# A hybrid decoder step on one core: input loads, chunk order, gelus and state decay put in other places

## The chip, the cores and the metric

The kernel runs on one core of a Trainium2 chip. The metric is the device time of one execution in microseconds; the kernel before took 1114.2 us, the median of three runs (1113.9 to 1114.36). The engines named here are TensorE (PE, matmuls), VectorE (DVE), ScalarE (ACT), GpSimd (POOL) and SyncE (SP, which issues most transfers). They run side by side, each in its own order of instructions, and wait for each other by semaphores.

## The reference

One decoder layer over 536 tokens: 16 meta tokens and 512 prompt tokens of one sequence, and one new token for each of 8 running samples. All of it is float32.

```python
xn = rmsnorm(x);  proj = xn @ w_in                  # columns z (1024), xbc (1536), dt (16), u (1024)
xbc = silu(causal_conv(xbc));  dt = softplus(dt + dt_bias)
# SSD group: 16 heads of 64, state 128, chunks of 128 tokens
for chunk c:
    y_diag = ((C B^T) * exp(segment sums) * dt) @ x  # inside the chunk
    y_off  = (C @ H) * exp(cumulated decay)          # from the state H before the chunk
    H      = decay_of_chunk * H + B^T @ (decayed x)
y_ssd = rmsnorm((y_diag + y_off + D x) * silu(z))
# S5 group: 64 groups of 16 channels, complex diagonal state of 64
y = gelu(Re(C h) + D u);  y = y * sigmoid(y @ w_glu + b_glu);  y_s5 = rmsnorm(y)
x = x + concat(y_ssd, y_s5) @ w_out
x = x + experts(rmsnorm(x))                          # 32 SwiGLU experts, two per token in one of 4 groups
y = rmsnorm(x)                                       # and the new states
```

The states of the eight samples are updated too: each is multiplied by its decay, gets an outer product added, and is read out against C.

## The kernel before, in words

**Wide blocks.** The input projection and the first S5 gate (GLU) are 36 blocks of 128 output features over all 536 tokens, `wide(0)` to `wide(35)`: 0 to 7 make u, 8 to 19 make xbc, 20 to 27 make z, and 28 to 35 multiply the gelu output `yg` by `w_glu`. A block is 64 float32 matmuls (recorded as x32), takes its weights (512 KB) from one of three ring buffers, which `ring_load(w)` on SP fills once block w-3 is done, and writes two PSUM banks, which ScalarE then empties (`wide_free`). Blocks 20 to 27 all use banks 0 and 1; from block 28 on even ones use 0 and 1, odd ones 2 and 3.

**S5.** Eight tokens are done at a time through a Toeplitz matrix `Tm` of 64 groups. It is assembled by 32 small SP transfers, `toeplitz(r)` for r = 0 to 3 with eight pieces each (L406). GpSimd runs the recurrence over 66 steps meanwhile (L553 to L564, end marked by `h_done`). `state_outputs(first, n)` on TensorE (L768) then makes n rounds of four groups in PSUM banks 2 and 3, and VectorE adds each to the rest of y (L1651, `y5_ev`); round r waits for the addition of round r-2. Because y has another layout than the gate needs, SP stores it to `y_scr` in HBM, in two halves of nine transfers (`y_store`, L432), and loads it back (`y_load`, L436). Then ScalarE takes the gelus (L1209) and TensorE may begin block 28, tile by tile.

**SSD.** Each of five chunks (the last has 16 tokens) has four parts on TensorE: `ssd_a` (transposes L779, L781 and C B^T, L783), `ssd_b` (segment sums, L794, in banks 2 and 3), `ssd_y_off` (C @ H, L802) and `ssd_c` (y and the new state, L815 to L824). ScalarE takes `b_tokens`, then the exponentials `segment_exp` (L1176). VectorE scales the off-diagonal part (L1624, `yo_ev`), multiplies the masks (L1629), adds y (L1636, `y_ev`) and then decays the state `Hs` and adds to it (L1646, `st_ev`).

**Samples.** When the last state output is done, GpSimd loads 2 MB of rows of B and C and eight states of 512 KB (L576, L578). For each sample VectorE makes the product with C and its sum (`sample_c`, L1608); only then may GpSimd overwrite the state (L586, L587) and store it (L591).

**Out-projection and experts.** y is split into a high and a low float32r part (L1690); `project_block` (L911) starts when the gate blocks are out of PSUM and the low part of `y_ssd` is made. SP issues the first experts' weights on counts of the out-projection. Routing follows, then 32 experts whose 6 MB each stream through three buffers.

All orders are written out by hand, as the order of calls on each engine. Those around the change are the SP list (L409 to L448), the TensorE list from `ssd_b(0)` to `wide(35)` (L829 to L866), the ScalarE loop over chunks with the gelus behind it (L1197 to L1214) and the VectorE loop over chunks (L1611 to L1657).

Of the kernel before, what the change touches and what calls it, by code (L numbers as in the profile page):

```python
# [38 lines left out]
NP_ = META + SEQ  # L39
# [41 lines left out]
def build(nc, a):  # L81
    ctx = ExitStack()
    with ctx:
# [268 lines left out]
        def _(sp):  # L352
# [58 lines left out]
            toeplitz(0)  # L411
            toeplitz(1)
            ring_load(14)
            toeplitz(2)
            toeplitz(3)
            for w in range(15, 22):
                ring_load(w)
# [22 lines left out]
            for w in range(26, 29):  # L440
                ring_load(w)
# [5 lines left out]
            for w in range(29, 31):  # L447
                ring_load(w)  # L448
# [180 lines left out]
        def _(pe):  # L629
# [214 lines left out]
            wide(24)  # L844
            state_outputs(0, 8)
            ssd_a(2)
# [10 lines left out]
            wide(26)  # L857
            ssd_c(3)
            wide(27)
# [3 lines left out]
            wide(28)  # L863
            ssd_c(4)
            for w in range(29, 36):
                wide(w)  # L866
# [170 lines left out]
        def _(ac):  # L1037
# [159 lines left out]
            for c in range(5):  # L1197
                b_tokens(c)
                if c:
                    segment_exp(c)  # L1200
                if c < 4:
                    decays(c + 1)
                for w in ((21, 22), (23, 24), (25,), (26, 27), ())[c]:
                    z_evac(w)

            for i in range(8):
                if i % 4 == 0:
                    ac.wait_ge(yraw_ld[i // 4], 16)
                act_(yg[:, i, 0:NP_].rearrange("p (m j) -> p m j", j=J),  # L1209
                     yraw[:, i, 0:NP_].rearrange("p (j m) -> p m j", j=J), ACT.Gelu_apprx_tanh)  # L1210
                act_(yg[:, i, NP_:N], yraw[:, i, NP_:N], ACT.Gelu_apprx_tanh).then_inc(gelu_done, 1)
            for i in range(2):
                ac.wait_ge(wide_free[i], 14)
# [149 lines left out]
        def _(dv):  # L1363
# [9 lines left out]
            def tt(o, x, y, op):  # L1373
                link(V.tensor_tensor(o, x, y, op))  # L1374
# [237 lines left out]
            for c in range(5):  # L1612
# [9 lines left out]
                for g in range(2) if c else ():  # L1622
# [3 lines left out]
                                    bc(dE[0:n, c, 0, 8 * g:8 * g + 8], 2, HD), ALU.mult).then_inc(yo_ev, 1)  # L1626
                for g in range(2):
# [3 lines left out]
                if c == 4:  # L1631
                    sample_c(2)
                    sample_c(3)
# [6 lines left out]
                for g in range(2):  # L1640
# [3 lines left out]
                    else:  # L1644
                        tt(hs, hs, bc(dE[:, c, 1, 8 * g:8 * g + 8], 2, HD), ALU.mult)
# [7 lines left out]
                if c == 3:  # L1653
                    sample_c(0)
                    sample_c(1)
            for b in range(4, NS):
                sample_c(b)  # L1657
# [322 lines left out]
```

## Time and profile before

| what | us |
|---|---|
| median of three runs | 1114.2 |
| profiled execution | 1111.12 |
| its span | 1109.3 |
| TensorE busy in it | 995.4 (90%) |
| VectorE busy | 440.9 (40%) |
| ScalarE busy | 310.7 (28%) |
| GpSimd busy | 329.9 (30%) |
| mean granted TensorE clock | 0.961 of full speed |

The profile is of one execution. Its times are counted from the start of the span. Busy shares are means over the whole span, in which the stages differ: the last half (from 588 us on) is the experts, the first half the layer's two head groups and the out-projection. Register, branch and semaphore instructions are not counted as busy, and a few matmul records may be missing.

### The profile page before, as it was taken

To read this page: it belongs to the slowest core of one execution; us is meant where nothing else is said; L and a number is where in the kernel's file an instruction comes from. 1 tells how busy PE (TensorE), PEld (TensorE's weight loads), DVE (VectorE), ACT (ScalarE), POOL (GpSimd) and SP (SyncE) were. 2 spreads that over 40 slices of the span, in tenths; PEclk is the share of its full clock that TensorE was granted. 3 is DMA by queue.
4 is the path that set the end of the run, shared out by engine and by line. 5 is a ranking of instruction groups with operands and counts; after the bars stand their busy time and mean duration, and the time that the engine had idled before them with its cause. 6 is when DMAs were issued, how large, how long until landed. Compare 5 with 4: busy or idle time off the path is not lost.

```text
span 1109.3 us, 17059 instructions
## 1 busy us (share of the span) xinstructions
PE 995.4 (90%) x6472; PEld 708.7 (64%) x6473; DVE 440.9 (40%) x673; ACT 310.7 (28%) x595; POOL 329.9 (30%) x534
## 2 busy tenths in 40 slices
PE   6999989999999999999889999999987687998881
PEld 5889769786776788898676555555544344554440
DVE  6999874534345699952331111111111011111103
ACT  3025223543312535411312222222211211221223
POOL 1000888888023992000002222222222121221210
PEclk9999999999979899999959999999999999999996
DMA  7683261110629734346369999999999999999964
GB/s 266 121 144 67 49 133 39 39 60 22 104 84 267 237 123 151 106 191 264 141 246 324 396 400 367 351 390 398 397 395 409 388 419 412 411 418 415 423 278 161
DMA packets 73564, 277.54 MB, mean 250 GB/s; under 512 B 36952, under 2 KB 38872, under 8 KB 56496
## 3 DMA queue, kind: packets, MB, share of 16 engines
q1 hardware_dynamic: 63020, 252.67, 62.4%
q0 software_dynamic: 8720, 19.86, 6.5%
q10 hardware_dynamic: 1780, 4.41, 1.1%
q8 instruction: 29, 0.48, 0.2%
q14 instruction: 15, 0.12, 0.0%
HBM read 260.17 MB, written 25.61 MB: 258 GB/s over the span
## 4 chain that ended last, share of the span: by engine, by line
PE 51%; DMA 22%; DVE 18%; SPq 5%; issue 2%; ACT 1%; POOLq 0%; ACTq 0%; POOL 0%; DVEq 0%
DMA sb_arena<-w_up 19%; PE ps L649 9%; PE ps L1005 9%; PE ps L1019 7%; DVE sb_arena L1374 7%; PE ps L998 7%; PE ps L911 6%; SPq L406 2%; SPq L432 2%; PE ps L963 2%; PE ps L979 2%; PE ps L768 2%; PE ps L737 1%; PE ps L819 1%; DVE sb_arena L1506 1%
## 5 line engine op out<-in xcount | busy, mean ns | idle before, releaser
L649 PE MATMUL ps<-sb_arena 128*128 128x264 f32 (+1 forms) x1152 | 271.7, 396 | 15.7 <-DVE sb_arena L1417 8.9
L649 PEld LDWEIGHTS ps<-sb_arena 128*128 128x128 f32 x1152 | 221.1, 193 | 66.6 <-DMA sb_arena<-wi 13.8
L1875 DVE TENSOR_TENSOR sb_s5b<-sb_s5b,ps 128x256 f32<-128x256 f32 x36 | 22.4, 622 | 411.2 <-PE ps L1005 411.2
L1005 PE MATMUL ps<-sb_arena 128*64 128x256 f32 x1152 | 136.2, 391 | 21.2 <-DMA sb_arena<-w_up 21.2
L1019 PE MATMUL ps<-sb_arena 128*64 128x512 f32 x576 | 131.5, 598 | 20.5 <-DVE sb_arena L1879 20.5
L998 PE MATMUL ps<-sb_arena 128*64 128x256 f32 x1152 | 131.0, 380 | 15.8 <-DMA sb_arena<-w_gate 12.3
L998 PEld LDWEIGHTS ps<-sb_arena 128*64 128x64 f32 x1152 | 82.9, 137 | 74.4 <-DMA sb_arena<-w_gate 20.9
L1005 PEld LDWEIGHTS ps<-sb_arena 128*64 128x64 f32 x1152 | 84.3, 141 | 69.3 <-DMA sb_arena<-w_up 27.5
L1347 ACT ACTIVATE sb_kxf<-ps,sb_gate_of 64x512 f32<-64x512 f32 x36 | 24.6, 682 | 306.6 <-PE ps L1019 306.6
L1019 PEld LDWEIGHTS ps<-sb_arena 128*64 128x64 f32 x576 | 39.0, 136 | 89.9 <-issue 61.0
L605 POOL COPY sb_idc<-sb_tok_of 64x1 int32 x36 | 6.4, 177 | 281.0 <-DMA sum_scr<-sb_kxf,sb_rwc 249.6
L1374 DVE TENSOR_TENSOR sb_arena<-sb_arena 128x64 f32<-128x64 f32 (+12 forms) x86 | 83.2, 968 | 5.5 <-ACT sb_arena L1048 1.9
L616 POOL DMA_INDIRECT sum_scr<-sb_kxf,sb_rwc x36 | 52.6, 1460 | 30.4 <-POOL sb_rwc L613 30.4
L911 PE MATMUL ps<-sb_y_hi,sb_wo_hi 128*128 128x268 f32 x256 | 53.9, 292 | 4.8 <-DVE sb_arena L1743 2.6
L911 PE MATMUL ps<-sb_y_lo,sb_wo_hi 128*128 128x268 f32 x256 | 52.4, 286 | 0.0
L911 PE MATMUL ps<-sb_y_hi,sb_wo_lo 128*128 128x268 f32 x256 | 52.3, 286 | 0.0
L596 POOL DMA_INDIRECT sb_arena<-x_scr,sb_tok_of x4 | 3.8, 960 | 161.9 <-DVE sb_tok_of L1865 161.0
L911 PEld LDWEIGHTS ps<-sb_y_hi,sb_wo_hi 128*128 128x128 f32 x256 | 39.9, 188 | 8.8 <-issue 5.5
L608 POOL DMA_INDIRECT sb_arena<-x_scr,sb_idc x36 | 34.8, 968 | 30.2 <-POOL sb_idc L605 28.6
L979 PEld LDWEIGHTS ps<-sb_cst,sb_arena 64*128 64x128 f32 x288 | 34.5, 200 | 13.8 <-issue 13.8
L911 PEld LDWEIGHTS ps<-sb_y_lo,sb_wo_hi 128*128 128x128 f32 x256 | 39.9, 188 | 0.0
L911 PEld LDWEIGHTS ps<-sb_y_hi,sb_wo_lo 128*128 128x128 f32 x256 | 39.8, 188 | 0.0
(301 smaller groups left out, 1292.2 us busy)
## 6 DMA issues: line engine op xcount, KB each, us to landing
sb_arena<-w_gate SPq DMA_DIRECT2D x32, 2048.0 KB, 30.2
sb_arena<-w_up SPq DMA_DIRECT2D x32, 2048.0 KB, 32.8
sb_arena<-w_down SPq DMA_DIRECT2D x32, 2048.0 KB, 32.6
sb_arena<-wi SPq DMA_DIRECT2D x28, 512.0 KB, 4.0
sb_arena<-w_out SPq DMA_DIRECT2D x4, 2048.0 KB, 8.3
sb_arena<-wglu SPq DMA_DIRECT2D x8, 512.0 KB, 4.3
sb_arena<-ssm_in POOLq DMA_DIRECT2D x8, 512.0 KB, 15.4
o_ssm_s<-sb_arena POOLq DMA_DIRECT2D x8, 512.0 KB, 5.1
```

The lines of the kernel that those rows point to most:

```text
L406: sp.dma_start(Tm[16 * j:16 * j + 16, r::4, j:J, :], Kx[32 * r:32 * r + 16, :, 0:J - j, :]).then_inc(t_ld, 16)
L608: nc.gpsimd.indirect_dma_start(xg[u], None, x_scr, bass.IndirectOffsetOnAxis(ap=idc[u], axis=0), bounds_check=N - 1, oob_is_err=False).the ...
L616: nc.gpsimd.indirect_dma_start(sum_scr, bass.IndirectOffsetOnAxis(ap=rwc[u % 2], axis=0), yo[u % 2], None, bounds_check=N - 1, oob_is_err= ...
L649: last = mm(ps[:, b0 + h, 0:t1 - t0], ring[w % 3][:, k, :], src[:, k, t0:t1], start=k == 0, stop=k == KD - 1)
L911: last = mm(ps[:, 2 * (o % 2) + h, 0:HALF], w_[:, k, c:c + P], y_[:, k, HALF * h:HALF * h + HALF], start=k == 0 and j == 0, stop=k == KD - ...
L979: last = nc.tensor.transpose(ps[:, 2, k * T:(k + 1) * T], rows_[:, k::KD], cst[0:T, C_ID:C_ID + T])
L998: last = mm(ps[64 * r:64 * r + 64, 0, 0:256], xt[:, k, :], Wg[s][:, k, 256 * r:256 * r + 256], start=k == 0, stop=k == KD - 1)
L1005: last = mm(ps[64 * r:64 * r + 64, 1, 0:256], xt[:, k, :], Wu[s][:, k, 256 * r:256 * r + 256], start=k == 0, stop=k == KD - 1)
L1019: last = mm(ps[64 * r:64 * r + 64, 4, :], ht[:, k % 2, 64 * (k // 2):64 * (k // 2) + 64], Wd[s][:, k, 512 * r:512 * r + 512], start=k == 0 ...
L1347: act_(yo[u % 2][:, 0:512], ps[0:64, 4, :], ACT.Copy, scale=gate_of[0:64, bass.ds(q, 1)])
L1374: link(V.tensor_tensor(o, x, y, op))
L1875: V.tensor_tensor(hh.rearrange("p (j c) -> p c j", j=2), sg.rearrange("p (c j) -> p c j", j=2), ps[:, 1, 0:256].rearrange("p (c j) -> p c ...
```

## The change

SP issues the loads of blocks 14 and 15 between Toeplitz rounds, and that of block 28 behind the second y store and both y loads. TensorE does chunk 2's `ssd_a` ahead of the first state outputs, block 27 ahead of chunk 3's `ssd_c`, block 28 ahead of all of chunk 4, and block 29 ahead of chunk 4's `ssd_c`, with a wait for both scaled off-diagonal parts since block 29 writes their banks. ScalarE does chunk 4's `b_tokens` and exponentials behind the gelus, and the gelus read contiguously and write with stride, where they read with stride and wrote contiguously. VectorE decays each half of the state as soon as its off-diagonal part is scaled, and does the samples' products in other places: 0 to 2 in chunk 3 ahead of y, 3 to 5 behind chunk 3's state, 6 and 7 in chunk 4 ahead of y (before: 0 and 1 behind chunk 3's state, 2 and 3 in chunk 4 ahead of y, 4 to 7 behind it).

```diff
@@ SP @@
             toeplitz(0)
+            ring_load(14)
             toeplitz(1)
-            ring_load(14)
+            ring_load(15)
             toeplitz(2)
             toeplitz(3)
-            for w in range(15, 22):
+            for w in range(16, 22):
                 ring_load(w)
...
             y_store(0)
-            for w in range(26, 29):
+            for w in range(26, 28):
                 ring_load(w)
             y_store(1)
             sp.wait_ge(y5_st[0], 16 * 9)
             y_load(0)
             sp.wait_ge(y5_st[1], 16 * 9)
             y_load(1)
-            for w in range(29, 31):
+            for w in range(28, 31):
                 ring_load(w)
@@ TensorE @@
             wide(24)
+            ssd_a(2)
             state_outputs(0, 8)
-            ssd_a(2)
             pe.wait_ge(y5_ev, 8)
...
             wide(26)
+            wide(27)
             ssd_c(3)
-            wide(27)
+            wide(28)
             ssd_a(4)
             ssd_b(4)
             ssd_y_off(4)
-            wide(28)
+            pe.wait_ge(yo_ev, 8)
+            wide(29)
             ssd_c(4)
-            for w in range(29, 36):
+            for w in range(30, 36):
                 wide(w)
@@ ScalarE @@
-            for c in range(5):
+            for c in range(4):
                 b_tokens(c)
                 if c:
                     segment_exp(c)
-                if c < 4:
-                    decays(c + 1)
-                for w in ((21, 22), (23, 24), (25,), (26, 27), ())[c]:
+                decays(c + 1)
+                for w in ((21, 22), (23, 24), (25,), (26, 27))[c]:
                     z_evac(w)
...
-                act_(yg[:, i, 0:NP_].rearrange("p (m j) -> p m j", j=J),
-                     yraw[:, i, 0:NP_].rearrange("p (j m) -> p m j", j=J), ACT.Gelu_apprx_tanh)
+                act_(yg[:, i, 0:NP_].rearrange("p (m j) -> p j m", j=J),
+                     yraw[:, i, 0:NP_].rearrange("p (j m) -> p j m", j=J), ACT.Gelu_apprx_tanh)
                 act_(yg[:, i, NP_:N], yraw[:, i, NP_:N], ACT.Gelu_apprx_tanh).then_inc(gelu_done, 1)
+            b_tokens(4)
+            segment_exp(4)
@@ VectorE, in the loop over chunks @@
                                     bc(dE[0:n, c, 0, 8 * g:8 * g + 8], 2, HD), ALU.mult).then_inc(yo_ev, 1)
+                    tt(Hs[:, 8 * g:8 * g + 8, :], Hs[:, 8 * g:8 * g + 8, :], bc(dE[:, c, 1, 8 * g:8 * g + 8], 2, HD), ALU.mult)
...
-                if c == 4:
-                    sample_c(2)
-                    sample_c(3)
+                for b in ((0, 1, 2) if c == 3 else (6, 7) if c == 4 else ()):
+                    sample_c(b)
                 dv.wait_ge(y_mm, c + 1)
...
-                        tt(hs, hs, bc(dE[:, c, 1, 8 * g:8 * g + 8], 2, HD), ALU.mult)
                         last = V.tensor_tensor(hs, hs, pg, ALU.add)
...
                 if c == 3:
-                    sample_c(0)
-                    sample_c(1)
-            for b in range(4, NS):
-                sample_c(b)
+                    for b in range(3, 6):
+                        sample_c(b)
```

## Rows read from the trace of the kernel before

**Rows 1.** The page's head.
```profile
span 1109.3 us, 17059 instructions
```

**Rows 2.** Chain that ended last: start us, us, what; two of its pieces.
```profile
588.39 3.67 PE ps L998 x32
...
795.09 39.20 DMA sb_arena<-w_up
```

**Rows 3.** Order of time of SP's queue: start, us, engine, line, what.
```profile
128.11 14.12 SPq L406 DMA_DIRECT2D sb_arena<-sb_kxf  x16
...
157.77 20.95 SPq L374 DMA_DIRECT2D sb_arena<-wi  x5
```

**Rows 4.** Order of time of TensorE; in brackets idle us before it, and releaser.
```profile
161.95 16.41 PE L649 MATMUL ps<-sb_arena 128*128 128x264 f32 x64 [4.89 <-DMA sb_arena<-wi]
...
278.54 8.50 PE L768 MATMUL ps<-sb_arena 128*128 128x75 f32 x64
...
286.87 1.05 PE L779 MATMUL ps<-sb_cst,sb_arena 128*128 128x128 f32 x8
...
312.55 10.52 PE L768 MATMUL ps<-sb_arena 128*128 128x75 f32 x48 [1.29 <-DVE sb_arena L1651]
322.88 1.90 PE L779 MATMUL ps<-sb_cst,sb_arena 128*128 128x128 f32 x8
...
331.34 7.39 PE L649 MATMUL ps<-sb_arena 128*128 128x264 f32 x32
...
353.81 1.04 PE L779 MATMUL ps<-sb_cst,sb_arena 128*16 128x128 f32 x8
...
359.62 9.22 PE L649 MATMUL ps<-sb_arena 128*128 128x264 f32 x32 [1.32 <-ACT sb_arena L1211]
...
376.00 38.73 PE L649 MATMUL ps<-sb_arena 128*128 128x264 f32 x160
...
432.12 0.48 PE L911 MATMUL ps<-sb_y_hi,sb_wo_hi 128*128 128x268 f32 x2 [2.12 <-DVE sb_y_lo L1690]
```

**Rows 5.** Stretches: us, TensorE busy (instructions), granted clock, DMA share, GB/s.
```profile
162.00:178.00 16.00, 16.00 (x64) 0.89 0.23 79
...
316.00:319.00 3.00, 3.00 (x16) 0.50 0.00 0
...
331.00:346.00 15.00, 15.00 (x85) 1.00 1.04 321
```

**Rows 6.** Order of time of VectorE: decays of the state.
```profile
310.71 0.68 DVE L1374 TENSOR_TENSOR sb_kxf<-sb_kxf,sb_arena 128x512 f32<-128x512 f32 x1
...
376.11 2.49 DVE L1374 TENSOR_TENSOR sb_kxf<-sb_kxf,sb_arena 128x512 f32<-128x512 f32 x1 [1.62 <-PE ps L824]
```

**Rows 7.** Order of time of GpSimd.
```profile
273.66 1.60 POOL L564 TENSOR_TENSOR sb_s5b<-sb_s5b,sb_arena 128x512 f32<-128x512 f32 x1
...
324.16 7.05 POOL L578 DMA_DIRECT2D sb_arena<-ssm_in  x8
...
352.22 2.89 POOL L586 TENSOR_TENSOR sb_arena<-sb_arena,sb_eA 128x1024 f32<-128x1024 f32 x1 [15.62 <-DVE sb_ysm L1608]
```

**Rows 8.** SP's queue around y; last, the gate loads' times to landing.
```profile
323.60 25.00 SPq L432 DMA_DIRECT2D y_scr<-sb_arena  x8
...
349.18 6.94 SPq L436 DMA_DIRECT2D sb_arena<-y_scr  x2
356.16 0.98 SPq L374 DMA_DIRECT2D sb_arena<-wglu  x2
...
DMA to landing us min/median/max: 3.9/4.3/9.6
```

**Rows 9.** Order of time of ScalarE.
```profile
356.49 1.28 ACT L1209 ACT_TABLE_LOAD   x1
358.20 1.17 ACT L1209 ACTIVATE sb_arena<-sb_arena 128x528 f32<-128x528 f32 x1 [0.43 <-DMA sb_arena<-y_scr]
```

**Rows 10.** Groups by line and shape: busy us, mean ns, idle before.
```profile
L1106 ACT ACTIVATE sb_arena<-ps 128x264 f32<-128x264 f32 x16 | 10.2, 637 | 3.9 <-PE ps L681 3.9
```

## The prediction

> **What bounds the kernel now.** I read the page first, then the chain that ended last, then the order of time of each engine where the change lies. The profiled execution took 1111.12 us, 1.8 us more than its span of 1109.3 us [rows 1]; the median of the three timed runs is 1114.2 us. All sums are made on the profiled execution and the difference is put on the median. The chain shows that from 588 us on the experts run without a gap, first at TensorE's pace and then at that of their weights' transfers [rows 2]; the transfers too begin on counts of TensorE's out-projection. So a microsecond won or lost before the out-projection goes to the end in full. It begins at 432.12 us, after a wait of 2.1 us for the low part of y [rows 4]. I call that moment B and ask where the change puts it. Until then TensorE is nearly always busy, so three things count: its gaps, the stretches in which its granted clock is 0.50 (1.2 GHz, otherwise 2.4 GHz), and the S5 y, which goes out to HBM and back between two matmul blocks.
>
> **Loads amid the Toeplitz pieces.** SP issues two rounds of pieces in 14.1 us, one load, two more rounds, and only at 157.77 us the load of block 15 [rows 3]. TensorE stands 4.89 us for it, and then its clock is low for a while: blocks 15 and 16 take 16.41 us [rows 4] where two blocks take 14.8 (2 x 7.39, the block at 331.34), at a mean granted clock of 0.89 [rows 5]. In the new order that load is issued after the second round, about 143 us, and lands (about 4 us) long before 157. The queue's other transfers move by one issue, 0.6 us. Gain: 4.9 + 1.6 = 6.5 us. VectorE's convolutions, which run beside, could eat up to 3 us of it; I take none, since nothing on TensorE waited for them there.
>
> **Chunk 2's first part ahead of the state outputs.** These need GpSimd's recurrence, which ends at 273.66 + 1.60 = 275.3 us [rows 7] and isn't moved. TensorE reached them at 278.54 [rows 4], with 3.3 us in hand; 6.5 us earlier would be 272.0. The moved part (286.87 to 288.4, 1.55 us) is put into this hole, so it ends at 273.6 and TensorE stands 1.7 us. The state outputs take 8.4 us, to 283.7. What follows (the moved part hid it) is the last addition of VectorE, 0.7 us, so the chunk goes on at 284.4 instead of 288.4. Of the 6.5 us, 4.0 are left.
>
> **State decay ahead.** After chunk 2 VectorE did two decays of 0.68 us each [rows 6] before it could add the first state output; TensorE waited 1.29 us for that, to 312.55 [rows 4]. With the decays earlier the wait is about 0. In this kernel that wait stands just before a low clock: after it the granted clock is 0.50 [rows 5], the six remaining rounds take 10.52 us (1.75 each) against 8.50 for eight (1.06 each), and the transposes 1.90 against 1.05 [rows 4]. If the clock stays up, as it did in the same work at 278.54, the rounds save 4.2 us and the rest of chunk 3's front (322.88 to 331.34, 8.5 us against 6.9) 1.5. Gain 7.0 us; bounds 1.3 and 7.0. The last state output is then ready 4.0 + 1.3 + 4.2 = 9.5 us earlier, and block 26 starts 11.0 us earlier, at 320.3.
>
> **Products of the samples.** In VectorE they were partly on the way to B (four samples, a product and a sum each, behind the last state). They go into its waits for TensorE and cost nothing there. But GpSimd waited 15.6 us for the first product [rows 7] and now has it about 12 us sooner: its first store of 0.5 MB falls into the y transfers, where the DMA moved 321 GB/s with all engines busy [rows 5]. I charge 0.5 MB / 321 GB/s = 1.6 us, bounds 0 and 3.2 (two stores).
>
> **The way of y.** From the last state output (323.60) SP needs 25.0 us to issue the eight stores, since GpSimd's loads of 6 MB begin at the same moment [rows 7, 8]. The first load back is issued at 349.18, and the first gelu starts at 358.20 [rows 9]: 34.6 us in all. GpSimd's loads wait for the same event, so this stays: the gelu starts at 314.1 + 34.6 + 1.6 = 350.3, the first is done at 351.5. The gelus change their access, from strided reads with contiguous writes to the reverse; one takes 1.17 us now. The nearest strided write in the trace, 264 elements from PSUM, takes 637 ns [rows 10], or about 1.1 to 1.3 us for 528. I keep 1.17, bounds 0.65 and 1.6; even at 1.6 the last is done with block 28, as below, so the cost is 0 to 1.
>
> Block 28 needs its weights too. Their load used to be issued at 301, before y; now it stands behind both y loads, where that of block 29 stood (356.16 [rows 8]), so at 348.3. Such loads land after 3.9 to 9.6 us, 4.3 in the middle [rows 8]; with 1 MB of y ahead of it I take 6. Block 28 starts at 354.3, bounds 351.5 and 358.
>
> **TensorE before and after block 28.** It has blocks 26 and 27 (7.2 each, with 0.7 between, since both use one bank and ScalarE must empty it) and chunk 3's outputs (8.0). It is done at 343.4 and stands 11 us. Before, chunk 4's front filled such a hole, and it waited only 1.32 us for the gelu [rows 4]. This is the price of the new order. From block 28 on:
> - block 28: 7.3 instead of the 9.2 of now, when it went at the gelus' pace, plus a low clock after the hole. The stretch after the wait at 157 cost 1.6; I take 2.5, bounds 1.6 and 3.4. Sum 9.8.
> - chunk 4's front: 4.5 now (353.81 to 358.3). The exponentials now follow gelus, so they need a table load of 1.28 [rows 9]: +1.4. Block 29 waits until VectorE has scaled both off-diagonal parts with one decay between, 0.65 + 0.7 + 0.65 = 2.0. Sum 7.9; 9.7 if the decay takes the 2.49 us seen beside GpSimd [rows 6].
> - block 29: 7.3, and a low clock after two gaps of about 1 us; bounds 0 and 3.4, I take 1.0. Sum 8.3.
> - chunk 4's outputs 6.2, blocks 30 to 35 43.4. After these tiny matmuls five blocks took 38.73 us [rows 4] where 5 x 7.23 = 36.2 would do, and the end of chunk 4's outputs took 1.0 more than its like in chunk 3: a low clock again, 3.4 us, which remains. Sum 53.0.
> - ScalarE's last evacuation, 0.9.
>
> B = 354.3 + 79.9 = 434.2, against 432.1: 2.1 us later, of which VectorE's spare time behind B gives back 0.1. The y path now bounds B, no longer VectorE: it has the last state about 1.5 us after chunk 4's outputs and then some 20 us in hand. So what is won before y, 9.5 us, is spent on the later weights and store (5 us), the low clock, the table load and the wait for the scaled parts. The profiled execution would be 1111.1 + 2.0 = 1113.1, the median 1114.2 + 2.0 = 1116.2.
>
> The Trainium skill, "ScalarE: Activation LUTs", "What ACT_TABLE_LOAD costs", gives a load about 1283 ns and a drain of about 1380 ns behind it, which speaks against this change. The trace agrees on the load, 1.28 us; between it and the gelu there were only 0.43 us, put down to the y transfer, so it shows no such drain [rows 9]. By the page's figures the sum would be 1.4 us more, 1117.6.
>
> **The rivals.**
> - Slower: the clock falls in the first state outputs. The 1.7 us in which TensorE waits for GpSimd stand before small matmuls, as did the 1.29 us at 311, where the clock fell. Then eight rounds take 1.75 instead of 1.06, +5.5 us, all ahead of y: 1121.7. It decides if the wait is longer than what the clock forgives. For it: the same work after a shorter gap. Against it: dense transposes ahead of the gap, and 1.32 us at 358 did not bring the clock down.
> - Faster: the y path has less in its way. The block's weights land with the gelus (-2.8), the clock is low only 1.6 after the hole (-0.9) and not before block 29 (-1.0), and one of two further things holds: the store doesn't disturb (-1.6), or chunk 4's outputs no longer bring the clock down (-3.3). Sum -6.3 to -8.0: about 1109. For it: each is within what the rows show. Against it: they must come together.
> - The change doesn't do what it says in chunk 2: the clock falls there although the wait is gone. Then 5.7 us of the 7.0 are missing: 1121.9.
>
> **How the numbers follow.** A measurement of this kernel tells changes from about 0.2% (2.2 us). Forecast case 0.38, own range 1112 to 1120: 0.06 faster, 0.20 same, 0.12 slower. Slower rival 0.25: 0.02 same, 0.23 slower. Faster rival 0.32: 0.29 faster, 0.03 same. Third 0.05, slower. Sum: faster 0.35, same 0.25, slower 0.40. The range 1107 to 1123 takes in both rivals.
>
> **What would show it.** Right: no gap near 157 us; the state outputs start near 275.3 after a gap of 1 to 2 us; full clock in the second state outputs; a hole of about 11 us on TensorE ahead of block 28, its weights landing last; a table load between chunk 4's front and block 29; B near 434. Wrong: a last state output later than 316 (low clock), or a hole under 7 us, which would mean y comes back faster than 34.6 us and the kernel is faster.

## The result, and the profile after

The changed kernel took 1123.36 us in the median of four executions, against 1114.05 us for the kernel before on the same chip: the ratio is 1.0072, with a 95% interval of 1.0047 to 1.0098. In a second series (a0 below) it took 1120.58 us in the median of seven, ratio 1.0056 (1.0033 to 1.0078). By these ratios it is slower by 0.56 to 0.72%, 6 to 8 us. (The ratios are not the quotients of the two medians, which lie 9.3 and 5.4 us apart.)

Its times are spread far more widely than the bound of 2 us I argued with: 1116.7 to 1127.3 us in the first series, 1117.1 to 1125.8 in the second. The execution that was profiled first is the fastest of all eleven, 1116.72 us with a span of 1114.9 us. The profile of the second series is of an execution of 1125.81 us, the slowest of its seven. The recorded expectations call these two the good and the common execution; here the second is called the bad one, since six of the eleven executions lie at 1122.3 us or above and five at 1120.6 or below, and none near the median was profiled. The two profiles lie near the two ends of the spread.

First profile, of the good execution: TensorE in order of time (start, us, what; in brackets the idle us before it and what ended it). The rows answer to [rows 4]:
```profile
158.05 14.62 PE L650 MATMUL ps<-sb_arena 128*128 128x264 f32 x64
189.76 24.70 PE L650 MATMUL ps<-sb_arena 128*128 128x264 f32 x96
...
277.60 8.50 PE L769 MATMUL ps<-sb_arena 128*128 128x75 f32 x64
286.66 3.80 PE L795 MATMUL ps<-sb_arena 128*128 128x512 f32 x8 [0.56 <-DVE sb_arena L1654]
...
307.35 8.58 PE L769 MATMUL ps<-sb_arena 128*128 128x75 f32 x64
...
356.04 9.05 PE L650 MATMUL ps<-sb_arena 128*128 128x264 f32 x32 [9.65 <-DMA sb_arena<-wglu]
...
368.36 0.39 PE L795 MATMUL ps<-sb_arena 16*16 16x64 f32 x4 [1.67 <-ACT sb_arena L1179]
...
372.91 9.14 PE L650 MATMUL ps<-sb_arena 128*128 128x264 f32 x32 [0.84 <-DVE sb_arena L1628]
...
389.83 45.35 PE L650 MATMUL ps<-sb_arena 128*128 128x264 f32 x192
436.18 0.48 PE L914 MATMUL ps<-sb_y_hi,sb_wo_hi 128*128 128x268 f32 x2 [1.00 <-issue]
```

Second profile, of the bad execution (a0, 1125.81 us), the same rows from the first state outputs on:
```profile
276.02 13.90 PE L769 MATMUL ps<-sb_arena 128*128 128x75 f32 x64 [1.98 <-POOL sb_s5b L565]
290.48 6.71 PE L795 MATMUL ps<-sb_arena 128*128 128x512 f32 x8 [0.56 <-DVE sb_arena L1654]
...
314.08 8.59 PE L769 MATMUL ps<-sb_arena 128*128 128x75 f32 x64
...
362.32 10.41 PE L650 MATMUL ps<-sb_arena 128*128 128x264 f32 x32 [9.20 <-DMA sb_arena<-wglu]
...
381.85 9.18 PE L650 MATMUL ps<-sb_arena 128*128 128x264 f32 x32 [3.37 <-DVE sb_arena L1628]
...
445.15 0.49 PE L914 MATMUL ps<-sb_y_hi,sb_wo_hi 128*128 128x268 f32 x2 [0.99 <-issue]
```

What the reader is to see there. In both, the wait of 4.89 us at 157 is gone. In the second profile TensorE then stands 1.98 us for GpSimd's recurrence, and the 64 small matmuls behind it take 13.90 us instead of 8.50, and the segment sums 6.71 instead of 3.80. In the first profile that does not happen, for an odd reason: a low clock had come earlier, at the end of the tiny cumulative sums ahead of 189.76, and blocks 17 to 19 took 24.70 us instead of the 21.95 of the second profile. TensorE came to chunk 2's first part 3.7 us later (276.06 against 272.34) and to the state outputs at 277.60, 0.6 us after GpSimd's recurrence had ended (276.97), and kept its clock. The granted clock (the third number from the end of each row) of the two stretches says so, first of the first profile:
```profile
190.00:195.00 5.00, 5.00 (x12) 3.80 (x13) 0.97 (x5) 0.00 (x0) 4.06 (x13) 0.50 0.00 0
277.00:286.00 9.00, 9.00 (x71) 8.87 (x69) 3.27 (x7) 0.38 (x1) 1.15 (x2) 1.00 0.09 33
```
and then of the second:
```profile
276.00:290.00 14.00, 13.90 (x64) 13.69 (x64) 3.31 (x8) 0.00 (x0) 1.14 (x2) 0.50 0.06 21
```

The out-projection, moment B, starts at 436.18 us in one and at 445.15 in the other; it was 432.12 before [rows 4]. The end follows B, though not to the microsecond: 678.7 and 678.9 us from B to the end of the span, 677.2 before. That 677.2 is the shortest of all profiles here (the other kernels have 678.1 to 679.8). The profile on which the prediction's sums were made is itself of a fast execution: 1111.12 us, where the same kernel's medians in the later series were 1114.8 to 1115.6 and its fastest executions 1111.1 to 1112.1. So some 1.5 us of the difference between the profiles lie behind B.

SP's queue and ScalarE of the first profile, around y (the answer to [rows 8, 9]): the weights of blocks 28 to 30 are issued behind the two loads of y, and gelu tiles follow each other at 1.01 us instead of 1.15.
```profile
316.47 23.68 SPq L433 DMA_DIRECT2D y_scr<-sb_arena  x8
340.19 1.89 SPq L434 DMA_DIRECT2D y_scr<-sb_arena  x1
342.12 6.50 SPq L437 DMA_DIRECT2D sb_arena<-y_scr  x2
348.67 1.53 SPq L374 DMA_DIRECT2D sb_arena<-wglu  x3
```
```profile
339.11 1.28 ACT L1211 ACT_TABLE_LOAD   x1
351.49 1.18 ACT L1211 ACTIVATE sb_arena<-sb_arena 128x528 f32<-128x528 f32 x1 [11.10 <-DMA sb_arena<-y_scr]
352.53 1.15 ACT L1211 ACTIVATE sb_arena<-sb_arena 128x528 f32<-128x528 f32 x1
...
366.80 1.28 ACT L1179 ACT_TABLE_LOAD   x1
```

### The profile page after: what moved, and what is told of

It is laid out like the page before. It is cut to its first block, busy times and chain, and to the rows that moved or that the text cites. A ratio compares the mean times of both kernels' runs of the same rounds, so it can differ in the third digit from the quotient of the medians.

```text
span 1114.9 us, 17069 instructions
## 1 busy us (share of the span) xinstructions
PE 998.3 (90%) x6472; PEld 709.7 (64%) x6473; DVE 429.6 (39%) x673; ACT 311.0 (28%) x596; POOL 322.4 (29%) x534
## 4 chain that ended last, share of the span: by engine, by line
PE 68%; DMA 22%; DVE 4%; SPq 2%; ACT 1%; issue 1%; ACTq 0%; POOLq 0%; POOL 0%; DVEq 0%
PE ps L650 23%; DMA sb_arena<-w_up 19%; PE ps L1008 8%; PE ps L1022 7%; PE ps L1001 7%; PE ps L914 6%; SPq L433 2%; PE ps L966 2%; PE ps L982 2%; PE ps L769 2%; PE ps L682 1%; PE ps L738 1%; PE ps L795 1%; PE ps L820 1%; PE ps L825 1%
## 5 line engine op out<-in xcount | busy, mean ns | idle before, releaser
L650 PE MATMUL ps<-sb_arena 128*128 128x264 f32 (+1 forms) x1152 | 274.9, 401 | 20.2 <-DMA sb_arena<-wglu 9.6
L650 PEld LDWEIGHTS ps<-sb_arena 128*128 128x128 f32 x1152 | 224.9, 196 | 71.3 <-DMA sb_arena<-wglu 10.5
L1378 DVE TENSOR_TENSOR sb_arena<-sb_arena 128x64 f32<-128x64 f32 (+12 forms) x86 | 80.8, 939 | 13.2 <-DMA sb_arena<-ssm_in 7.7
```

What stands on the lines that cost most here:

```text
L650: last = mm(ps[:, b0 + h, 0:t1 - t0], ring[w % 3][:, k, :], src[:, k, t0:t1], start=k == 0, stop=k == KD - 1)
```

## The experiments

Two theories stood against each other. By the first, the loss is made late: the order around chunk 4 opens a hole on TensorE, and the late weights widen it. By the second it is made by the clock: the time won at 157 us ends in a wait for GpSimd ahead of small matmuls, and the clock falls there. Both turned out to hold. Ratios are against the kernel before on the same chip in the same series.

| run | what it is | median us (executions) | ratio, 95% interval |
|---|---|---|---|
| a0 | changed kernel again | 1120.58 (7) | 1.0056 (1.0033 to 1.0078) |
| a_w28 | its block 28 weights early | 1117.49 (12) | 1.0012 (0.9995 to 1.0030) |
| a_front | its order around chunk 4 put back | 1113.75 (12) | 0.9981 (0.9961 to 1.0001) |
| a_early | both put back | 1111.30 (10) | 0.9957 (0.9936 to 0.9979) |
| a_noload | its Toeplitz loads put back | 1123.24 (5) | 1.0077 (1.0063 to 1.0090) |
| b_load | before + early loads | 1116.38 (12) | 1.0004 (0.9988 to 1.0021) |
| b_decay | before + state decay ahead | 1108.21 (5) | 0.9948 (0.9935 to 0.9961) |
| b_gelu | before + gelus' access | 1115.00 (12) | 0.9997 (0.9982 to 1.0011) |
| c_front2 | b_load + TensorE's wait filled | 1107.32 (5) | 0.9930 (0.9916 to 0.9944) |
| c_all | c_front2 + decay + gelus' access | 1100.98 (5) | 0.9885 (0.9869 to 0.9901) |
| d_samp | c_all + samples' products earlier | 1101.02 (6) | 0.9884 (0.9859 to 0.9910) |
| e_late | c_all + late order around chunk 4 | 1113.97 (12) | 0.9987 (0.9975 to 0.9999) |

### b_load: the early loads alone

The diff is the first hunk of the change and nothing else.

> The kernel before with the loads of blocks 14 and 15 amid the Toeplitz pieces and nothing else. Theory: the wait of 4.89 us at 157 goes and the clock stays up there, but TensorE then reaches the first state outputs at about 272 us, 3.3 us ahead of GpSimd's recurrence: 3.3 us are left, about 1111. Rival 1 (the wait of 3.3 us ahead of small matmuls brings the clock down, as that of 1.29 us at 311 did): 5.5 us are lost there, about 1116. Rival 2 (the low clock only moves, to 190 us, as in the changed kernel): 2.5 us are left, none of them at GpSimd's wait, about 1111.5, with the granted clock 0.50 near 190.

Rival 1 holds for the upper heap of executions. TensorE waited 3.90 us for GpSimd and the state outputs then took 13.65 us:
```profile
276.73 13.65 PE L769 MATMUL ps<-sb_arena 128*128 128x75 f32 x64 [3.90 <-POOL sb_s5b L565]
290.18 1.90 PE L780 MATMUL ps<-sb_cst,sb_arena 128*128 128x128 f32 x8
```
Its twelve times fall into two heaps, 1110.7 to 1111.9 us (four) and 1115.2 to 1119.2 us (eight). Only one execution, of the upper heap, has a profile, so that the lower heap is the one in which the clock held is an inference; its place is where the theory without a fall put it, 1111. On average an edit that removes a stall of 4.89 us is worth nothing.

### b_decay: the state decay alone

```diff
                                     bc(dE[0:n, c, 0, 8 * g:8 * g + 8], 2, HD), ALU.mult).then_inc(yo_ev, 1)
+                    tt(Hs[:, 8 * g:8 * g + 8, :], Hs[:, 8 * g:8 * g + 8, :], bc(dE[:, c, 1, 8 * g:8 * g + 8], 2, HD), ALU.mult)
...
-                        tt(hs, hs, bc(dE[:, c, 1, 8 * g:8 * g + 8], 2, HD), ALU.mult)
                         last = V.tensor_tensor(hs, hs, pg, ALU.add)
```

> The kernel before with the state decayed as soon as each off-diagonal part is scaled, and nothing else. Theory: the wait of 1.29 us ahead of the third of the second state outputs goes and the clock stays up in them: 7 us sooner at the last state output; TensorE and y are then both 7 us earlier: about 1107. Rival (the fall of the clock at 313 doesn't hang on the wait but on what TensorE did before): only the wait is won, about 1112.8.

The theory holds: 1108.21 us, 6.6 below the median of before in that series (by the ratio of 0.9948, 5.8 us). Two instructions of 0.68 us per chunk were moved. The second state outputs now run without a break at full clock, where they had needed 10.52 us for six of eight rounds [rows 4]:
```profile
309.21 8.58 PE L768 MATMUL ps<-sb_arena 128*128 128x75 f32 x64
...
427.05 0.48 PE L911 MATMUL ps<-sb_y_hi,sb_wo_hi 128*128 128x268 f32 x2 [1.00 <-ACT sb_arena L1244]
```

### c_front2: the same early loads, with the wait filled by real work

```diff
             wide(24)
-            state_outputs(0, 8)
             ssd_a(2)
-            pe.wait_ge(y5_ev, 8)
             ssd_b(2)
             ssd_y_off(2)
             wide(25)
+            pe.wait_ge(yo_ev, 4)
+            state_outputs(0, 8)
             ssd_c(2)
+            pe.wait_ge(y5_ev, 8)
             state_outputs(8, 8)
```
VectorE adds rounds 0 to 7 behind chunk 2's masks instead of behind chunk 1.

> The kernel before with the early loads, and on TensorE chunk 2's whole first part and block 25 ahead of the first state outputs (VectorE adds these rounds behind chunk 2's masks). Nothing else of the change. It takes away the wait for GpSimd (it ends at 277, the state outputs now come at 287) by real work instead of by a later start. Theory (the clock falls because of that wait): first state outputs in 8.5 us at full clock, the last state output about 5 us sooner than before: about 1109 to 1110, against 1116.4 with the early loads alone. Rival (the clock falls because TensorE has been busy since 158 without a pause, or by the small matmuls themselves): 13.7 us for the first state outputs as with the early loads alone, at or above 1114.

The theory holds, and by more than it said: 1107.32 us, 9 us (8 by the ratios) below b_load, which issues the same loads. The whole spread is 1105.2 to 1107.5. The first state outputs come at 285.72, GpSimd has been done for 10 us, and the clock stays up. The wait of 1.29 us ahead of the second ones, which this version keeps, still brings it down there:
```profile
285.72 8.51 PE L769 MATMUL ps<-sb_arena 128*128 128x75 f32 x64
...
305.61 10.52 PE L769 MATMUL ps<-sb_arena 128*128 128x75 f32 x48 [1.29 <-DVE sb_arena L1658]
```
So the same small matmuls, in the same kernel, run at 2.4 GHz without a gap ahead of them and at 1.2 GHz with one. It is the wait, not the matmuls, and not how long TensorE had been busy before: by 285.72 it had run since 157 with no wait above 0.44 us. c_front2 also changes what stands ahead of the first state outputs (block 25 instead of chunk 2's small matmuls). That this isn't the reason is shown by b_decay, which removes the wait and leaves TensorE's order as it was, and by a_noload below, where chunk 2's first part still stands ahead.

### a0: the changed kernel again

Nothing is edited.

> The changed kernel once more, unaltered, for the spread of its times and a second profile. Theory: its first profile (1116.7 us) was its rare good execution, in which the clock fell near 190 us, so that TensorE came later to the wait for GpSimd's recurrence and the first state outputs kept the full clock. Most executions are like the profiles of the three variants that issue these loads early: a wait of 2.3 us or more ahead of the first state outputs, 13.7 us for their 64 matmuls instead of 8.5: median 1122 to 1124, the best ones 6 us below. Rival: the executions above 1122 lose their time elsewhere (a later hole, the router): the second profile shows 8.5 us for the first state outputs at a time above 1121.

The profile is as expected (shown above: a wait of 1.98 us, 13.90 us). The median of 1120.58 is 1.4 us below the range I gave, since four of seven executions lay between 1117.1 and 1120.6 and three between 1124.5 and 1125.8. The good execution is thus not rare. Whether those around 1118 to 1121 had the wait or not is open, as none of them was profiled.

### a_noload: the changed kernel without its early loads

> The changed kernel with the loads of blocks 14 and 15 where they were before (after the second Toeplitz round, and after all four). Theory (what the early loads win at 157 us is lost at GpSimd's recurrence): TensorE comes to the first state outputs at about 280 us without a wait, they take 8.5 us, and the last state output is about 4.7 us sooner than with the early loads in the common execution: about 1118.7, and a narrow spread. Rival (the early loads are worth their 4.9 us or a part, and the loss is in the later parts alone): slower than the changed kernel, 1125 or more.

The mechanism is as expected (281.13 us, no wait, 8.51 us at full clock), and the spread is narrow, 1122.1 to 1124.0. The time is not: 1123.24 where I expected 1118.7. Its profile has B at 441.88, behind a hole of 9.77 us ahead of block 28 and 2.98 us ahead of block 29. It stands between the good execution (436.18) and the bad one (445.15), as its last state output does (319.5, against 315.9 and 322.7). I had worked from 1123.4 for the common execution; the upper executions lie at 1122 to 1127, so my base was about 2 us low. The rest, some 2 us, I can't place. The rival is not shown right either: the early loads are worth 0 to 3 us here (ratios 1.0077 without them, 1.0056 and 1.0072 with). What they win at 157 us is nearly all lost again.
```profile
281.13 8.51 PE L768 MATMUL ps<-sb_arena 128*128 128x75 f32 x64
...
359.69 10.16 PE L649 MATMUL ps<-sb_arena 128*128 128x264 f32 x32 [9.77 <-DMA sb_arena<-wglu]
```

### a_w28, a_early, a_front: late weights and late order, each with and without

In a_w28 only the place of `ring_load(28)` is before's:
```diff
-            for w in range(26, 28):
+            for w in range(26, 29):
                 ring_load(w)
             y_store(1)
...
-            for w in range(28, 31):
+            for w in range(29, 31):
```

> The changed kernel with the load of block 28's weights issued where it was before, ahead of the second y store. Theory (order at the gate): in the profile of the changed kernel block 28 began 3.3 us after its first gelu was done, since its weights landed at 355.99 us; with them there, TensorE's hole falls from 9.65 to about 6.5 us and the kernel gains 3 us: about 1120 in the median. Rival (low clock in the first half makes the loss): the hole costs little, because what is won is given back by a clock that stays low as long: under 1 us, about 1123.

In a_early everything from block 26 on is as before as well:
```diff
             wide(26)
-            wide(27)
             ssd_c(3)
-            wide(28)
+            wide(27)
             ssd_a(4)
             ssd_b(4)
             ssd_y_off(4)
-            pe.wait_ge(yo_ev, 8)
-            wide(29)
+            wide(28)
             ssd_c(4)
```
with ScalarE's loop over five chunks and the samples' products of before.

> The changed kernel with everything from block 26 on put back (TensorE's and ScalarE's order around chunk 4, block 28's weights, the samples' products); it keeps the loads amid the Toeplitz pieces, chunk 2's first part ahead of the state outputs, the state decay ahead and the gelus' new access. Theory (the loss is made by the late parts): the last state output comes some 8 us sooner than before, the chunk 4 front fills the hole again, block 28 starts about 353 instead of 359.6: 6 us faster than before, about 1108. Rival (the early parts bring their own low clock, seen at 190 us in the profile of the changed kernel and more in its slower executions): at or above the time before, 1114 to 1120.

In a_front the same is put back, but the weights stay late.

> The changed kernel with TensorE's and ScalarE's order around chunk 4 and the samples' products back as before, but block 28's weights still loaded behind y: it completes a table of four with the changed kernel, that with the weights early (1117.5) and that with both back (1111.3). Theory (the weights cost what they come after the gelu, whatever stands ahead of block 28): block 28 starts 3 to 4.6 us later than with both back: 1115 to 1116. Rival (with chunk 4's first part in the hole the late weights are hidden): 1111.3, within 1 us.

One row of each, block 28: a_w28, a_early, a_front.
```profile
358.37 9.15 PE L650 MATMUL ps<-sb_arena 128*128 128x264 f32 x32 [4.64 <-ACT sb_arena L1213]
```
```profile
356.51 4.15 PE L650 MATMUL ps<-sb_arena 128*128 128x264 f32 x16 [1.09 <-ACT sb_arena L1212]
363.01 4.22 PE L650 MATMUL ps<-sb_arena 128*128 128x264 f32 x16 [2.35 <-ACT sb_arena L1212]
```
```profile
364.03 9.57 PE L650 MATMUL ps<-sb_arena 128*128 128x264 f32 x32 [7.45 <-DMA sb_arena<-wglu]
```
By the medians the weights cost 2.5 us in the old order (1113.75 against 1111.30) and 3 to 6 us in the new one (1120.58 or 1123.36 against 1117.49); by the ratios 2.7 us, with an uncertainty of some 3, and 5 to 7. The order, with the samples' products that go with it, costs 6.2 us with early weights (1117.49 against 1111.30) and 7 to 10 with late ones. In a_w28 the hole fell from 9.65 to 4.64 us, more than the 3 us expected; a part of that is that the first gelu came 33.2 us after SP's second store instead of 35.0. In a_front the times alone would not tell the rival (hidden by chunk 4's first part) from the theory, whose 1115 to 1116 they miss by over 1 us. The rows do: the weights, issued at 355.75 right behind y's two loads, landed 8.3 us later, and a hole of 7.45 us is left that they end, since chunk 4's first part fills only 4.5 us. So the rival falls. In a_early theory and rival each got a piece: it is faster than before, but 3.5 us and not 6, since the clock fell in the first state outputs there too (13.71 us in its profile, behind a wait of 2.34).

### b_gelu: the gelus' access alone

> The kernel before with the gelus' access turned (contiguous reads, strided writes), and nothing else. Theory: the gelus' pace falls from 1.15 to 1.01 us a tile, as in the profile of the changed kernel, and block 28, which goes at their pace, ends about 1 us sooner; TensorE is then kept waiting by VectorE's low part of y instead, so nothing or 1 us of it is seen in the end: 1113.5 to 1115. Rival (a strided write costs more than a strided read where ScalarE is beside GpSimd's and VectorE's work): slower by over 1 us.

As the theory has it. The starts of the tiles are 1.04 and 1.01 us apart, and nothing of it is seen in the end. Before they were 1.17 and 1.14 apart (358.20 [rows 9], 359.37, 360.51). Three rows of b_gelu, then one of before:
```profile
360.01 1.17 ACT L1209 ACTIVATE sb_arena<-sb_arena 128x528 f32<-128x528 f32 x1
361.05 1.15 ACT L1209 ACTIVATE sb_arena<-sb_arena 128x528 f32<-128x528 f32 x1
362.06 1.16 ACT L1209 ACTIVATE sb_arena<-sb_arena 128x528 f32<-128x528 f32 x1
```
```profile
359.37 1.15 ACT L1209 ACTIVATE sb_arena<-sb_arena 128x528 f32<-128x528 f32 x1
```

### c_all: the good parts together

c_front2 with the diff of b_decay and the gelus' access of the change.

> The same with the state decay ahead and the gelus' new access: all parts of the change that the experiments so far speak for, TensorE's order from block 26 on as before. Theory (the gains add where no wait is in the way): 6.6 us for the decay, as it had alone, on top of the last: 1102 to 1104. Rival (the way of y back from HBM or VectorE becomes the bound, and part of the gain is spent in a wait ahead of block 28): 1106 or more, with a hole of over 3 us there.

1100.98 us, 1.15% (12.8 us) faster than the kernel before, and 1.7 to 2% faster than the changed one. It is the fastest kernel of the study with d_samp. The theory (1102 to 1104) holds, by 1 us more than it said: the gains of c_front2 and b_decay add up, and the wait ahead of block 28 is 2.5 us. From 155 us to 345 us the granted clock never falls (behind that wait it does, to 0.50 from 347 to 350):
```profile
155.00:275.00 120.00, 119.51 (x667) 95.46 (x665) 59.70 (x133) 47.67 (x126) 100.09 (x255) 1.00 0.16 49
275.00:345.00 70.00, 69.02 (x389) 50.83 (x388) 36.72 (x62) 16.62 (x52) 18.69 (x17) 1.00 0.68 167
```
```profile
302.19 8.58 PE L769 MATMUL ps<-sb_arena 128*128 128x75 f32 x64
...
346.97 9.40 PE L650 MATMUL ps<-sb_arena 128*128 128x264 f32 x32 [2.52 <-ACT sb_arena L1213]
...
419.60 0.48 PE L913 MATMUL ps<-sb_y_hi,sb_wo_hi 128*128 128x268 f32 x2 [2.95 <-DVE sb_y_lo L1697]
```

### d_samp: the samples' products earlier

```diff
-                if c == 4:
-                    sample_c(2)
-                    sample_c(3)
+                for b in ((0, 1, 2) if c == 3 else (3, 4) if c == 4 else ()):
+                    sample_c(b)
...
-                if c == 3:
-                    sample_c(0)
-                    sample_c(1)
-            for b in range(4, NS):
+            for b in range(5, NS):
```

> The fastest version so far (early loads, chunk 2's first part and block 25 ahead of the first state outputs, state decay ahead, gelus' access) with three samples' products ahead of chunk 3's y, where VectorE waited 9.2 us for TensorE, and two in chunk 4. It waited 2.95 us at the out-projection for VectorE's low part of y. Theory (a product taken off the chain behind the last state is worth its 2.4 to 3 us there): 1098 to 1099. Rival (GpSimd's first store of 0.5 MB, which waits for the first product, comes 5 us sooner and falls into the y transfers, as I charged 1.6 us for in the prediction): gelus later by 1.6 us or more, no gain or a loss, 1101 to 1103.

No gain in the median, and the interval is ±2.8 us, so the timing alone settles nothing. In the profiles one half of the argument appears: the out-projection no longer waits for the low part of y (0.99 us against 2.95). The other half is not shown. The first gelu does start 35.7 us after SP begins the second store of y (312.07 to 347.75), where c_all had 34.4 (311.30 to 345.66), and GpSimd's first store was issued at 339.36, 1.9 us behind SP's first load of y, instead of 6.1 us behind it. But in both profiles of the changed kernel, in a_w28 and in a_noload it was issued 1.6 to 1.8 us behind that load, and there the same stretch took 33.2 to 35.0 us; where the store comes later it took 32.9 to 34.6. The spread from run to run is as large as the cost that was looked for.
```profile
347.75 1.16 ACT L1211 ACTIVATE sb_arena<-sb_arena 128x528 f32<-128x528 f32 x1 [2.16 <-DMA sb_arena<-y_scr]
```
```profile
339.36 0.93 POOL L592 DMA_DIRECT2D o_ssm_s<-sb_arena  x1 [0.30 <-POOL sb_arena L588]
```

### e_late: the late order on the fast version

The diff is the change's order on TensorE from block 26 on and on ScalarE, put onto c_all.

> The fast version (early loads, chunk 2's first part and block 25 ahead of the first state outputs, state decay ahead, gelus' access; 1101.0) with the late order of the change on TensorE and ScalarE alone: blocks 27 and 28 ahead of chunk 3's outputs and chunk 4, chunk 4's exponentials behind the gelus, block 29 ahead of its outputs. Block 28's weights early, samples' products as before. Theory (the order has a price of its own: a hole ahead of block 28 since chunk 4's first part no longer fills it, a table load on the way, a wait for both scaled parts): the hole grows from 2.5 to about 6.5 us, 1.7 us for the exponentials and 1 to 3 us ahead of block 29 come on top, less the low clock that it had anyway: 1106 to 1108. Rival (the loss of 6 us seen between the two variants of the changed kernel comes from its samples' products or from the low clock of the state outputs, not from this order): within 2 us of 1101.

The theory is right in kind and too small: 1113.97 us, 13 us more than c_all (11 by the ratios). The rows say where:
```profile
346.43 9.85 PE L650 MATMUL ps<-sb_arena 128*128 128x264 f32 x32 [4.79 <-ACT sb_arena L1214]
...
359.55 0.39 PE L795 MATMUL ps<-sb_arena 16*16 16x64 f32 x4 [1.67 <-ACT sb_arena L1180]
...
364.80 9.06 PE L650 MATMUL ps<-sb_arena 128*128 128x264 f32 x32 [2.07 <-DVE sb_arena L1629]
...
416.00 16.27 PE L650 MATMUL ps<-sb_arena 128*128 128x264 f32 x64 [3.46 <-ACT sb_arena L1249]
433.27 0.49 PE L915 MATMUL ps<-sb_y_hi,sb_wo_hi 128*128 128x268 f32 x2 [1.00 <-ACT sb_arena L1249]
```
Block 28 starts at the same time as in c_all (346.43 and 346.97). Blocks 26 and 27 and chunk 3's outputs stand ahead of it in both; what changed is that chunk 4's first part, 4.5 us of work that fitted into the wait for y, now stands behind it. The gap is no longer a place in which anything useful stands. I had left out the wait at 416: VectorE, which still did four samples' products behind the last state, made the gated y_ssd late; ScalarE's squares of it waited 13.87 us for VectorE, the evacuation of a gate block stood behind them, and TensorE waited 3.46 us and then took 16.27 for two blocks instead of 14.6.
```profile
412.84 2.27 ACT L1232 ACTIVATE sb_arena<-sb_arena 128x536 f32<-128x536 f32 x4 [13.87 <-DVE sb_arena L1679]
415.02 0.46 ACT L1248 ACTIVATE sb_arena<-ps,sb_pf 128x264 f32<-128x264 f32 x1
```
The changed kernel, which has two products in chunk 4, ahead of its y, and none behind its state, has no such wait in either profile. So its placing of the samples' products seems to be what its order needs; the two were not tried the other way round.

## Why the prediction came out as it did

The forecast was +2.0 us, and the kernel is slower by 6 to 8. Put on the forecast's base of 1114.2 us, the ratios make 1120.4 to 1122.2: inside the stated range of 1107 to 1123, at its upper end, and slower was the outcome given the largest chance, 0.40. But the range is wide because it takes in the rivals. What came is not the forecast case but, in the one profile from the upper half of the executions, the slower rival; and its 1121.7 is met partly by chance, as its price was too small (below). The steps, in the order of the prediction; good is the first profile, bad the second:

| step | predicted | good | bad |
|---|---|---|---|
| blocks 15 and 16 without wait or low clock | 6.5 won | 6.7 (no 4.89; 14.62 for 16.41) | 6.7 |
| wait for GpSimd | 1.7 | none | 1.98 |
| clock in the first state outputs | full | full, low at 190 instead | 0.50 |
| second state outputs | 8.5 us | 8.58 | 8.59 |
| SP's second store starts, on the last state output | 314.1 | 316.5 | 323.2 |
| SP's second store to first gelu | 36.2 with 1.6 for GpSimd's store | 35.0 | 34.0 |
| hole ahead of block 28, ended by its weights | 11 | 9.65 | 9.20 |
| ScalarE's table load ahead of the sums | 1.4 | 1.67 | 1.67 |
| block 29 waits for VectorE | about 1 | 0.84 | 3.37 |
| block 28 starts | 354.3 | 356.0 | 362.3 |
| block 28 | 9.8 | 8.9 | 10.3 |
| chunk 4's front with its waits | 7.9 | 8.0 | 9.3 |
| block 29 | 8.3 | 9.1 | 9.1 |
| chunk 4's outputs to block 35 | 53.0 | 53.2 | 53.2 |
| last evacuation | 0.9 | 1.0 | 1.0 |
| B | 434.2 | 436.2 | 445.2 |

From "block 28 starts" on, the rows are the terms whose sum is B.

- **The step that failed is "The state outputs take 8.4 us, to 283.7".** I had written the fall of the clock behind a wait of 1.7 us as the slower rival and gave it 0.25, against 0.38 for the forecast case. The runs put it the other way: with a wait of 1.98 to 3.90 us there, all five profiles of kernels that had it (a0, a_w28, a_early, a_front, b_load) show 13.65 to 13.93 us for the 64 matmuls. Without the wait they take 8.51 (c_front2, a_noload). In the good execution the step held only by luck, since an unforeseen low clock at 190 us delayed TensorE until GpSimd was done. The argument against it in the prediction, that 1.32 us ahead of block 28 had not brought the clock down [rows 4], weighed a single case too heavily.
- **How much of the miss it is** can be read from a_early. The early parts were forecast to bring block 26 forward by 11.0 us; alone they make the kernel 3.5 to 5 us faster, and in a_early's profile block 26 starts only 2.9 us earlier (328.46 against 331.34), behind the low clock. The late parts were forecast to cost 13.1 us (11.0 won, B 2.1 later); they cost 11 to 13 (ratios 0.9957 against 1.0056 and 1.0072). So the late side of the sum was about right, and what is missing is missing on the early side.
- **The rival's price was too small.** I took 5.5 us for the eight rounds. The segment sums behind them cost another 2.9 (6.71 against 3.80), so from the state outputs' start to block 25 it is 22.8 us against 14.5 (276.02 to 298.84, 277.60 to 292.11): 8.3 us.
- **A low clock that I had not foreseen** is the one at 190 us in the good execution, 2.75 us, behind tiny matmuls and no wait. It stood in no other profile of a kernel with the early loads. So a wait is not the only thing behind which the clock falls.
- **Late weights, hole, table load and tail** came within 2 us of their terms each, apart from block 29's wait in the bad execution, and the hole was ended by the transfer named. The weights' price, 2.8 us in the prediction's sum (block 28 at 354.3, first gelu done at 351.5), is 2.5 to 7 us by a_w28 and a_front.
- **State decay ahead**: 7.0 predicted, 5.8 to 6.6 measured alone.
- **GpSimd's store** was charged 1.6 us. It was issued when the sum said, amid the transfers of y (343.80, between SP's two loads at 342.12 and 348.2), and SP's second store to the first gelu took 35.0 and 34.0 us against 34.6 before. No run shows a cost of its own; d_samp does not show one either.
- **Block 29's wait** was bounded by 9.7 us for chunk 4's front if the decay is slow beside GpSimd. The bad execution comes near it, 9.3 us, and the decay is only a part of that: 1.79 us for the decay between the two scalings and 3.00 for the product ahead of them, which took 1.21 in the good one.

The Trainium skill bears on two of these. Its page "TensorE: Matmul & The Clock Gate", section "HAM oscillation — how this bites in real kernels", says that a wait between pieces of matmul work makes TensorE begin the next piece at the low clock. This case agrees: 3.90 us of wait, then 0.50 of full speed. It goes further than the page's example, whose waits for a transfer are longer: here 1.29 us ahead of small matmuls was enough, while 1.32 us ahead of block 28 [rows 4] was not. Its section "The HAM clock gate" says that the cost of such a spell differs between runs of one kernel. The trace agrees as far as it goes: the same two blocks 15 and 16, behind a wait of 4.2 to 5.0 us each time, took 16.41 us (before, b_decay), 17.09 (a_noload) and 17.20 (b_gelu). The drain of about 1380 ns that "ScalarE: Activation LUTs" puts behind a table load is not seen: in the changed kernel the load at 366.80 took 1.28 us and the first exponential started at 368.09.

What stays open: why the clock fell at 190 us in one execution and not in the others, what the executions between the two profiles looked like, some 2 us of a_noload, and the share of the samples' products in the difference between a_w28 and a_early, which was not tried apart.

## What to carry to other kernels

A stall that is removed is won only if no later wait takes its place, and in this kernel a wait of 1.3 to 4 us ahead of small matmuls cost twice: itself, and 5 to 8 us at the lower clock behind it. Fill such a wait with work that is there anyway, and hold back or move the engine's short work rather than let it start after a gap; here that turned a gain of nothing (b_load) into 8 us (c_front2). Before moving the filler out of a hole, see what else will stand in it, and take two profiles of a kernel whose times lie in two heaps before explaining either.

## What the runs showed of the hardware

- The same 64 matmul records of 128x75 took 8.50 to 8.59 us at a granted clock of 1.00 and 13.65 to 13.93 at 0.50, the same in every kernel. A gap of 1.29 us was enough, each time, ahead of the second state outputs.
- Kernels with a wait of 2 to 4 us ahead of the first state outputs had spreads of 8 to 10 us over 7 to 12 executions. Without it a_noload, b_decay and c_front2 had 1.8 to 2.3 us over five each, but c_all 4.7 over five, d_samp 6.5 over six, b_gelu and e_late 5.1 and 5.2 over twelve, and the kernel before 4.3 to 8.9 over 12 to 27. So a wide spread alone is no sign of that wait.
- A low clock also followed shorter waits ahead of a block of 128x264 (block 29 of the good execution, behind waits of 1.67 and 0.84 us around chunk 4's tiny matmuls: 9.14 us for 7.39, granted clock 0.59 from 372.9 to 377), and the tiny matmuls of chunk 4's outputs with no wait at all (0.58 from 390 to 394).
- Gelus with contiguous reads and strided writes followed each other at 1.01 us a tile, with strided reads and contiguous writes at 1.14 to 1.19, though the profile gives each instruction 1.14 to 1.21 in both: the gain is in how closely they follow.
- A weight load of 512 KB issued right behind the two loads of y (1.1 MB each, the first still under way) landed 7.3 to 8.3 us later in four profiles (the changed kernel's two, a_noload, a_front), against 4.3 in the middle before [rows 8].
